# Constants first, rows in two parts, modulation tiles interleaved one pair ahead, and all four early column groups multiplied directly in fp32

## The chip, the cores and the metric

The kernel runs on one core of one Trainium2 chip. The metric is the device time of one execution in microseconds (us). The core has a tensor engine (PE, whose weight loads are listed as PEld), a vector engine (DVE), a scalar engine (ACT), GpSimd (POOL) and a sync engine (SP). Each of them takes its own instructions in order; they wait for one another through semaphores only. Transfers between HBM and on-chip memory are issued by SP, ACT and POOL and carried by 16 DMA engines.

## The reference

Two transformer-like blocks over 256 positions and width 2048, all in fp32. What matters here is how the first block begins:

```
mod = silu(c) @ w_ada + b_ada                 # 2048 -> 12288, one row
sh_a, sc_a, gt_a, sh_f, sc_f, gt_f = split(mod, 6)
h = rmsnorm(x, g_pre_attn) * (1 + sc_a) + sh_a
proj = h @ w_in                               # 2048 -> 6144: qa ka va qb kb vb
qa, ka, qb, kb = rope(...)                    # two attentions, then w_out
x = x + gt_a * rmsnorm(mix @ w_out)
# gated feed-forward, then the second block (mLSTM + convolution), a final norm
```

The projection can't begin before the row `mod` is known for the columns of `h` that it uses, and `mod` is itself a product with a large matrix (`w_ada`), done on the vector engine.

## The kernel before, in words

**Streamed weights.** All weights come as chunks of 1 MB, 128 partitions of 8 KB, into `RAW`, a ring of four slots (`RAWS = 4`). There are two kinds. A chunk of kind "A" holds the columns of `w_ada` for 128 values of `mod`: DVE multiplies it with the broadcast row `silu(c)` and sums (`ada_chunk`, line 1586), and the slot is free. A chunk of kind "W" holds two halves of 1024 columns of a projection. SP issues the loads in the order of the list that `first_body` returns, and before each it waits until the chunk four places earlier has been consumed (`slot_wait`).

**Halves.** A half, numbered h, is multiplied with one pair of k-tiles (2 x 128 rows of the contraction) of the activations for one group of 512 output columns. In the usual way ("split") ACT writes a rounded high part `HI` (line 648), DVE writes the rest `LO = RAW - HI` (line 1576), and PE makes 12 matmuls of 512 columns in the fp32r format: `XH*HI`, `XL*HI` (lines 1175, 1176) and `XH*LO` (line 1184). In the "direct" way ACT copies the raw half to `WHOLE` (line 645), DVE only writes one word so that the semaphore order stays (line 1573), and PE makes 4 matmuls of 512 columns in full fp32 with the unsplit `XT` (line 1199). Before, only group 3 of the first four groups is direct.

**The beginning.** Halves 0 to 31 are the first four column groups (`EARLY = 4`), walked k-pair by k-pair: for each of the eight pairs n, four A chunks give shift and scale of its two k-tiles, `first_scale(n)` (line 1815) finishes them, ACT's `x_pair(n)` (lines 763, 764) modulates `XT` and rounds to `XH`, DVE's `x_low(n)` (line 1821) makes `XL`, and then two W chunks hold the pair's four halves, one for each group. From half 32 on groups are walked one after the other, each with all eight pairs, always split; the attention's rotations, scores and products stand between the halves at places written out by hand (`ROPE_AT`, `QK_TURN_AT`). From chunk 18 on an A chunk follows nearly every W chunk. The other sections (feed-forward, down projection, second block) follow in the same ring.

**Start.** ACT issues the row `c` and five small loads (positions, `INV`, `COL`, `BCOL`, `IDENT`), SP the first A chunk and all of `x` as one transfer. ACT sums the squares of both row tiles (line 680), normalizes both (lines 743, 744), PE turns them with `IDENT` (line 1244), ACT copies them to `XT` (line 747). DVE computes the rotation angles (`angles`, lines 1790 to 1802) between the third and the fourth A chunk.

Of the kernel before, what the change touches and what calls it, by code (L numbers as in the profile page):

```python
# [348 lines left out]
def build(nc, x, c_rows, pos_cols, cols, bias_cols, lambda_q1, lambda_k1, lambda_q2, lambda_k2,  # L349
          b_in_2, normf_w_2, w_mod, w_first, w_ffn, w_down, w_second, w_gates, b_gates, k_ident, k_inv, k_mask_a, k_mask_b,  # L350
# [2083 lines left out]
```

## Time and profile before

| | us |
|---|---|
| median of 3 runs | 2419.84 |
| lowest, highest | 2418.53, 2421.32 |
| the profiled execution's own time | 2416.39 |
| its span | 2414.6 |
| PE busy | 2319.4 (96%) |
| DVE busy | 1828.0 (76%) |
| ACT busy | 1120.2 (46%) |

The profile is of one execution. The span runs from its first to its last recorded instruction; the time holds 1.8 us more around it. In all views "us" counts from the start of the span. Busy time of PE overlaps between pipelined matmuls; where PE is the bound, the distance from one start to the next is what counts. Records of a direct matmul appear twice (8 for the 4 matmuls of a half).

### The profile page before, as it was taken

The page shows a single profiled execution, that of the slowest core. Times are in us where ns is not written, and L with a number is a line of the kernel's source. Part 1 is how long each engine was busy: PE and PEld are TensorE (multiplying, and loading weights), DVE is VectorE, ACT ScalarE, POOL GpSimd, SP SyncE. Part 2 cuts the span into 40 slices and gives each one's busy share as a digit, 9 for nine tenths or more (in the row PEclk, how much of TensorE's full clock was granted, in tenths as well). Part 3 has the DMA queues.
Part 4 walks back from the last instruction along what each step waited for, and adds up shares of the span by engine and source line. Part 5 has one row for each costly group of instructions (what it writes and reads, how often), then busy time and mean ns, then how long its engine had stood idle before and what let it go on. Part 6 is the DMA issues. An engine that isn't in the chain of part 4 may idle for free.

```text
span 2414.6 us, 26091 instructions
## 1 busy us (share of the span) xinstructions
PE 2319.4 (96%) x10236; PEld 1898.1 (79%) x10236; DVE 1828.0 (76%) x2447; ACT 1120.2 (46%) x1470; POOL 16.7 (1%) x31
## 2 busy tenths in 40 slices
PE   4789999999999999999989999999999999999998
PEld 3557778778888888888868888888888888888887
DVE  5878988877878888887665567898778696555875
ACT  4334557465434444444464334444445544444453
POOL 0000000000000000000000000000000000000000
PEclk9899999999999999999989999999999999999999
DMA  8987788977788777888835655556566658555553
GB/s 314 363 322 268 279 295 334 367 266 286 276 251 327 279 280 279 302 331 318 300 137 190 231 190 197 176 203 205 205 202 206 208 196 252 208 192 192 192 192 122
DMA packets 88363, 599.51 MB, mean 248 GB/s; under 512 B 10416, under 2 KB 10816, under 8 KB 17072
## 3 DMA queue, kind: packets, MB, share of 16 engines
q1 hardware_dynamic: 85520, 588.94, 68.4%
q0 software_dynamic: 1712, 7.19, 0.9%
q8 instruction: 81, 1.33, 0.2%
q10 hardware_dynamic: 1008, 1.71, 0.2%
q14 instruction: 42, 0.34, 0.0%
HBM read 595.66 MB, written 2.13 MB: 248 GB/s over the span
## 4 chain that ended last, share of the span: by engine, by line
PE 87%; DVE 5%; DMA 3%; ACT 2%; issue 1%; DVEq 0%; ACTq 0%
PE PS L1159 20%; PE PS L1175 18%; PE PS L1184 18%; PE PS L1176 18%; PE PS L1164 10%; DMA RAW<-in_w_mod 2%; DVE RAW L1586 2%; DVE LO L1576 2%; DMA RAW<-in_w_first 1%; ACT HI L648 1%; PE PS L1290 1%; PE PS L1505 0%; ACT R L763 0%; DVE X L1663 0%; PE PS L1254 0%
## 5 line engine op out<-in xcount | busy, mean ns | idle before, releaser
L648 ACT ACTIVATE HI<-RAW 128x1024 fp32r<-128x1024 f32 x800 | 843.8, 1059 | 1109.9 <-PE PS L1184 659.3
L1576 DVE TENSOR_TENSOR LO<-RAW,HI 128x1024 fp32r<-128x1024 f32 x800 | 975.4, 1223 | 473.3 <-ACT HI L648 469.5
L1175 PE MATMUL PS<-HI,XH 128*128 128x512 f32 x2144 | 856.2, 399 | 37.1 <-ACT HI L648 28.1
L1176 PE MATMUL PS<-HI,XL 128*128 128x512 f32 x2144 | 843.3, 393 | 0.0
L1184 PE MATMUL PS<-LO,XH 128*128 128x512 f32 x2144 | 581.0, 392 | 0.3 <-DVE LO L1576 0.3
L1175 PEld LDWEIGHTS PS<-HI,XH 128*128 128x128 f32 x2144 | 407.2, 190 | 131.2 <-DVE XL L1821 33.7
L1184 PEld LDWEIGHTS PS<-LO,XH 128*128 128x128 f32 x2144 | 406.8, 190 | 87.3 <-DVE LO L1576 1.4
L1176 PEld LDWEIGHTS PS<-HI,XL 128*128 128x128 f32 x2144 | 407.8, 190 | 82.7 <-issue 0.2
L1159 PE MATMUL PS<-HI,XH 128*128 128x512 f32 x1056 | 326.3, 390 | 3.7 <-issue 2.3
L1159 PE MATMUL PS<-HI,XL 128*128 128x512 f32 x1056 | 325.9, 390 | 0.0
L1164 PE MATMUL PS<-LO,XH 128*128 128x512 f32 x1056 | 284.5, 390 | 0.0
L1614 DVE STREAM_TRANSPOSE R<-R 32x256 f32<-32x256 f32 (+1 forms) x608 | 230.9, 380 | 12.7
L1586 DVE CUSTOM_DVE_ANT_0 RAW<-RAW,BIAS 128x2048 f32<-128x2048 f32 x96 | 218.5, 2287 | 25.0 <-DMA RAW<-in_w_mod 13.5
L1159 PEld LDWEIGHTS PS<-HI,XH 128*128 128x128 f32 x1056 | 197.8, 188 | 44.8 <-issue 2.5
L1164 PEld LDWEIGHTS PS<-LO,XH 128*128 128x128 f32 x1056 | 198.8, 188 | 41.4
L1159 PEld LDWEIGHTS PS<-HI,XL 128*128 128x128 f32 x1056 | 198.5, 188 | 41.5
L1586 DVE CUSTOM_DVE_ANT_0 RAW<-RAW,R 128x2048 f32<-128x2048 f32 x48 | 109.9, 2289 | 0.5
L763 ACT ACTIVATE R<-R,MOD,SCALE 128x256 f32<-128x256 f32 x16 | 9.6, 599 | 80.2 <-DVE SCALE L1815 80.0
L1244 PE MATMUL PS<-IDENT,R 128*128 128x128 f32 x32 | 5.0, 332 | 28.5 <-DMA IDENT<-in_k_ident 28.5
L2234 DVE TENSOR_TENSOR R<-PS,BIAS 128x1024 f32<-128x1024 f32 x24 | 29.2, 1216 | 0.0
L1199 PE MATMUL PS<-R 128*128 128x512 f32 x64 | 28.7, 592 | 0.0
L1244 PEld LDWEIGHTS PS<-IDENT,R 128*128 128x128 f32 x32 | 4.8, 178 | 28.5 <-DMA IDENT<-in_k_ident 28.5
(246 smaller groups left out, 857.7 us busy)
## 6 DMA issues: line engine op xcount, KB each, us to landing
RAW<-in_w_second SPq DMA_DIRECT2D x208, 1024.0 KB, 4.8
RAW<-in_w_mod SPq DMA_DIRECT2D x144, 1024.0 KB, 5.8
RAW<-in_w_ffn SPq DMA_DIRECT2D x88, 1024.0 KB, 4.9
RAW<-in_w_first SPq DMA_DIRECT2D x64, 1024.0 KB, 6.5
RAW<-in_w_down SPq DMA_DIRECT2D x44, 1024.0 KB, 5.0
BIAS<-in_b_in SPq DMA_DIRECT2D x40, 256.0 KB, 5.2
R<-mod_rows POOLq DMA_DIRECT2D x3, 1024.0 KB, 9.8
X<-in_x SPq DMA_DIRECT2D x1, 2048.0 KB, 14.2
```

Of the source, the lines that this page charges most:

```text
L648: act.activation(HI[:, (it["half"] + hf) % HLS, :], whole, ACT.Copy).then_inc(s.hi_ready, 1)
L1159: pe.matmul(PS[:, bank_of(u, cc), :], x, HI[:, slot, cc * 512:(cc + 1) * 512], start=first and x is xh, stop=False)
L1164: m = pe.matmul(PS[:, bank_of(u, cc), :], XH[:, slot_k, u * P:(u + 1) * P], LO[:, slot, cc * 512:(cc + 1) * 512], start=False, stop=last)
L1175: pe.matmul(PS[:, bank + u, :], XH[:, 2 * n + kk, rows], hi, start=start and kk == 0, stop=False)
L1176: pe.matmul(PS[:, bank + u, :], XL[:, 2 * n + kk, rows], hi, start=False, stop=False)
L1184: m = pe.matmul(PS[:, bank + u, :], XH[:, 2 * n + kk, u * P:(u + 1) * P], lo, start=False, stop=stop and kk == 1)
L1199: m = pe.matmul(PS[:, bank + u, :], XT[:, 2 * n + kk, u * P:(u + 1) * P], as_it_is(h)[:, kk * 512:(kk + 1) * 512], start=start and kk == 0 ...
L1290: ins = pe.matmul(PS[:, 5, m * S:m * S + nk], QT[2 * m][rows, j, u * P:(u + 1) * P], QT[2 * m + 1][rows, j, 0:nk], start=True, stop=True, ...
L1576: dve.tensor_tensor(LO[:, slot, :], RAW[:, it["slot"], hf * 1024:(hf + 1) * 1024], HI[:, slot, :].bitcast(F32), ALU.subtract).then_inc(s.l ...
L1586: dve.tensor_tensor_reduce(w, w, C_ROW if a < ADA_OF_C else C_ROW_2, 1.0, 0.0, ALU.mult, ALU.add, MOD[:, a:a + 1]).then_inc(s.ada_step, 1)
L1614: m = dve.transpose(columns(b, a), rows(a, b))
L2234: dve.tensor_tensor(dst, y, bias, ALU.add).then_inc(s.group_out, 1)
```

## The change

It does six things.

1. `DIRECT` holds all four early groups: halves 0 to 31 all take the direct way. The four slots of `WHOLE` are now shared by four consecutive halves instead of four halves of group 3.
2. `first_body`: four A chunks, then for each pair n two A chunks of the next pair ahead of each of its two W chunks (none at the last pair).
3. `COL`, `BCOL`, `IDENT` and `INV` come as one tile `SMALLS`, issued first on ACT's queue; the row `c` moves from ACT's queue to the head of SP's.
4. `x` comes as two transfers; its squares start when the first has landed. Row tile 1 is normalized by DVE instead of ACT.
5. `angles` moves from behind the third A chunk to behind the fourteenth, `lambdas` from behind the sixth chunk of the list to behind the tenth A chunk, ACT's `tables` from half 5 to half 14.
6. PE's first two pairs of turns of rotated columns stand one half earlier.

```
-DIRECT = (3,)
+DIRECT = (0, 1, 2, 3)
...
-QK_TURN_AT = [(33, 34), (35, 36), (37, 38), (39, 40), (58, 60), (66, 68), (74, 76), (82, 84)]
+QK_TURN_AT = [(32, 33), (34, 35), (37, 38), (39, 40), (58, 60), (66, 68), (74, 76), (82, 84)]
...
 def first_body():
-    body = []
+
+    body = [("A",)] * 4
     for n in range(8):
-        body += [("A",)] * 4 + [("W", 2 * n), ("W", 2 * n + 1)]
+        ahead = [("A",)] * (2 if n < 7 else 0)
+        body += ahead + [("W", 2 * n)] + ahead + [("W", 2 * n + 1)]
...
+            sp.dma_start(C_ROW, c_rows[0:1, :].to_broadcast([P, D])).then_inc(s.c_in, 16)
...
                     if it["j"] == 0:
-                        sp.dma_start(X[:], x[0].rearrange("(u p) d -> p u d", p=P)).then_inc(s.x_in, 16)
+                        for u in range(NT):
+                            sp.dma_start(X[:, u, :], x[0, u * P:(u + 1) * P, :]).then_inc((s.x_in, s.x_in_1)[u], 16)
...
-            act.dma_start(C_ROW, c_rows[0:1, :].to_broadcast([P, D])).then_inc(s.c_in, 16)
+            act.dma_start(SMALLS[:], smalls).then_inc(s.small_in, 16)
             act.dma_start(POSI[:], pos_cols).then_inc(s.pos_in, 16)
-            act.dma_start(INV, k_inv.to_broadcast([P, 96])).then_inc(s.pos_in, 16)
-            act.dma_start(COL[:], cols).then_inc(s.small_in, 16)
-            act.dma_start(BCOL[:], bias_cols).then_inc(s.small_in, 16)
-            act.dma_start(IDENT[:], k_ident).then_inc(s.ident_in, 16)
...
-            act.activation(XN[:, 0, :], X[:, 0, :], ACT.Copy, scale=RSTD[:, 0:1])
-            act.activation(XN[:, 1, :], X[:, 1, :], ACT.Copy, scale=RSTD[:, 1:2]).then_inc(s.rows_normed, 1)
+            act.activation(XN[:, 0, :], X[:, 0, :], ACT.Copy, scale=RSTD[:, 0:1]).then_inc(s.rows_normed, 1)
...
-                if h == 5:
+                if h == 14:
                     tables()
...
-                    dve.memset(SMALL[:, 175:176], 0.0).then_inc(s.lo_ready, 1)
+                    dve.memset(READ[:, h:h + 1], 0.0).then_inc(s.lo_ready, 1)
...
                 dve.reciprocal(RSTD, ROOT).then_inc(s.rstd_ready, 1)
+                dve.wait_ge(s.rstd_ready, 1)
+                dve.tensor_scalar(XN[:, 1, :], X[:, 1, :], RSTD[:, 1:2], None, ALU.mult).then_inc(s.row_1, 1)
...
-                    if it["j"] == 1:
+                    if it["ada"] == 1:
+                        first_columns()
                         first_rstd()
-                    if it["j"] == 2:
+                    if it["ada"] == 13:
                         angles()
-                        first_columns()
...
-                    if it["j"] == 6:
+                    if it["ada"] == 9:
                         lambdas()
```

On the vector engine one pair in the middle of the beginning reads like this before (ISA with RAW is an A chunk, MEMSET the word of a direct half).

```order
L1586 ISA RAW,MOD<-RAW,BIAS 128x2048
L1586 ISA MOD 128x1
L1814 TENSOR_TENSOR MOD<-MOD,BCOL 128x4
L1815 SCALAR_TENSOR_TENSOR SCALE<-MOD,COL 128x2
L1821 TENSOR_TENSOR XL<-R,XH 128x512
L1576 TENSOR_TENSOR LO<-RAW,HI 128x1024 x3
L1573 MEMSET SMALL 128x1
L1586 ISA RAW,MOD<-RAW,BIAS 128x2048
```

And now, from the low part of a pair to the next one's.

```order
L1822 TENSOR_TENSOR XL<-R,XH 128x512
L1572 MEMSET READ 128x1 x2
L1585 ISA RAW,MOD<-RAW,BIAS 128x2048
L1585 ISA MOD 128x1
L1585 ISA RAW,MOD<-RAW,BIAS 128x2048
L1585 ISA MOD 128x1
L1815 TENSOR_TENSOR MOD<-MOD,SMALLS 128x4
L1816 SCALAR_TENSOR_TENSOR SCALE<-MOD,SMALLS 128x2
L1572 MEMSET READ 128x1 x2
L1585 ISA RAW,MOD<-RAW,BIAS 128x2048
```

The subtractions for LO are gone, and the scale of a pair no longer stands directly ahead of that pair's low part: two W halves, two A chunks and the next pair's work lie between.

On the sync engine the list of loads begins like this before (w_mod are the A chunks, w_first the W chunks).

```order
L543 DMA RAW<-in_w_mod 128x2048
L559 DMA X<-in_x 128x2x2048
L543 DMA RAW<-in_w_mod 128x2048 x3
L543 DMA RAW<-in_w_first 128x2048 x2
L543 DMA RAW<-in_w_mod 128x2048 x4
L543 DMA RAW<-in_w_first 128x2048 x2
```

And now.

```order
L554 DMA BIAS<-in_c_rows 128x2048
L544 DMA RAW<-in_w_mod 128x2048
L562 DMA X<-in_x 128x2048 x2
L544 DMA RAW<-in_w_mod 128x2048 x5
L544 DMA RAW<-in_w_first 128x2048
L544 DMA RAW<-in_w_mod 128x2048 x2
L544 DMA RAW<-in_w_first 128x2048
```

The row `c` stands at the head, and the first W chunk now comes after six A chunks instead of four.

On the tensor engine the beginning before repeats, eight times, three split halves and one direct; now it is the 32 turns of `x`, then 128 direct matmuls in one piece, and the first turn of rotated columns behind half 32.

```order
L1242 MATMUL PS<-SMALLS,R 128x128 x32
L1197 MATMUL PS<-R 128x512 x128
L1173 MATMUL PS<-HI,XH 128x512
L1174 MATMUL PS<-HI,XL 128x512
L1173 MATMUL PS<-HI,XH 128x512
L1174 MATMUL PS<-HI,XL 128x512
L1173 MATMUL PS<-HI,XH 128x512
L1174 MATMUL PS<-HI,XL 128x512
L1173 MATMUL PS<-HI,XH 128x512
L1174 MATMUL PS<-HI,XL 128x512
L1182 MATMUL PS<-LO,XH 128x512 x4
L1278 MATMUL PS<-SMALLS,R 128x128 x4
```

The last row is that turn; before, the first one stood behind half 33.

## Rows read from the trace of the kernel before

**Rows 1.** The page: busy time of PE, and PE in 40 slices.

```profile
PE 2319.4 (96%) x10236; PEld 1898.1 (79%) x10236; DVE 1828.0 (76%) x2447; ACT 1120.2 (46%) x1470; POOL 16.7 (1%) x31
...
PE   4789999999999999999989999999999999999998
```

**Rows 2.** Chain that ended last, pairs 6 and 7: start, us, what.

```profile
129.22 8.46 DMA RAW<-in_w_mod
...
140.43 0.61 ACT R L763
...
143.30 3.50 DVE LO L1576 x3
146.85 8.37 DMA RAW<-in_w_mod
```

**Rows 3.** Waits from 0 to 200 us: total, times, longest.

```profile
ACT R L763 <- DVE SCALE L1815: 80.0, 7, 12.2
PEld PS L1175 <- DVE XL L1821: 33.7, 7, 7.7
```

**Rows 4.** Windows: length, busy of each engine, PE clock, DMA share, GB/s.

```profile
0.00:10.00 10.00, 0.00 (x0) 0.00 (x0) 0.06 (x1) 1.64 (x2) 0.20 (x4) 1.00 0.82 302
10.00:20.00 10.00, 0.00 (x0) 0.00 (x0) 4.19 (x3) 7.05 (x7) 3.37 (x6) 1.00 0.97 389
20.00:30.00 10.00, 1.49 (x7) 1.49 (x8) 8.51 (x27) 4.10 (x3) 0.00 (x0) 1.00 1.00 318
...
135.00:140.00 5.00, 4.25 (x12) 1.87 (x10) 4.60 (x4) 0.00 (x0) 0.00 (x0) 1.00 1.00 421
140.00:145.00 5.00, 1.58 (x5) 1.31 (x6) 2.71 (x6) 4.50 (x6) 0.00 (x0) 0.89 1.01 424
145.00:150.00 5.00, 5.00 (x19) 4.00 (x18) 5.00 (x6) 1.11 (x2) 0.00 (x0) 0.77 0.69 234
...
450.00:500.00 50.00, 48.55 (x213) 39.59 (x212) 43.04 (x41) 22.39 (x33) 0.00 (x0) 1.00 0.96 367
```

**Rows 5.** Timeline of the start: start us, us, engine, line, op, idle before.

```profile
22.87 1.99 ACT L744 ACTIVATE R<-X,SMALL 128x2048 f32<-128x2048 f32 x1
23.75 0.17 DVE L1790 CAST SMALL<-POSI 128x2 f32<-128x2 int32 x1
28.52 5.03 PE L1244 MATMUL PS<-IDENT,R 128*128 128x128 f32 x32 [28.52 <-DMA IDENT<-in_k_ident]
29.69 2.28 DVE L1586 CUSTOM_DVE_ANT_0 RAW<-RAW,BIAS 128x2048 f32<-128x2048 f32 x1
34.78 2.00 ACT L648 ACTIVATE HI<-RAW 128x1024 fp32r<-128x1024 f32 x2
39.39 0.77 PE L1175 MATMUL PS<-HI,XH 128*128 128x512 f32 x1 [5.84 <-DVE XL L1821]
```

**Rows 6.** DVE groups by form: line, op, count, busy us, mean ns.

```profile
L1657 DVE TENSOR_SCALAR R<-X,SMALL 128x1024 f32<-128x1024 f32 x4 | 2.8, 748 | 0.0
```

**Rows 7.** Timeline of PE: starts of halves 29 and 30.

```profile
165.39 0.40 PE L1175 MATMUL PS<-HI,XH 128*128 128x512 f32 x1
...
168.12 0.39 PE L1175 MATMUL PS<-HI,XH 128*128 128x512 f32 x1
```

**Rows 8.** The chain at half 31, the last direct one.

```profile
171.00 3.43 PE PS L1199 x8
```

**Rows 9.** Timeline of DVE, PE, SP and ACT behind half 37.

```profile
190.36 0.69 DVE L1859 TENSOR_TENSOR R<-PS,R 128x512 f32<-128x512 f32 x1 [0.66 <-PE PS L1184]
...
196.46 1.09 PE L1279 MATMUL PS<-IDENT,R 128*128 128x128 f32 x4 [3.46 <-ACT R L776]
197.20 0.78 PE L1175 MATMUL PS<-HI,XH 128*128 128x512 f32 x1
...
198.68 0.33 SPq L543 DMA_DIRECT2D RAW<-in_w_first  x1
...
204.38 1.06 ACT L648 ACTIVATE HI<-RAW 128x1024 fp32r<-128x1024 f32 x1 [6.19 <-DMA RAW<-in_w_first]
```

More of the change, by code:

```diff
@@ L346, in turned_at, with build @@
     return (g, part) if 0 <= g < 11 else None
[L349 to L350 removed]
+def build(nc, x, c_rows, pos_cols, smalls, lambda_q1, lambda_k1, lambda_q2, lambda_k2,
+          b_in_2, normf_w_2, w_mod, w_first, w_ffn, w_down, w_second, w_gates, b_gates, k_mask_a, k_mask_b,
           k_mask_m, out):
@@ L369, in build @@
         X = sb("X", [P, NT, D])
-        IDENT = sb("IDENT", [P, P])
-        COL = sb("COL", [P, 146])
+        SMALLS = sb("SMALLS", [P, 514])
+        COL, BCOL, IDENT, INV = SMALLS[:, 0:146], SMALLS[:, 146:290], SMALLS[:, 290:418], SMALLS[:, 418:514]
         COL2 = COL[:, 96:114]
         MOD = sb("MOD", [P, ADA_CHUNKS])
-        BCOL = sb("BCOL", [P, ADA_CHUNKS])
         SCALE = sb("SCALE", [P, NK])
@@ L382, in build @@
         WIFL = sb("WIFL", [P, NK, 16], F32R)
+        READ = sb("READ", [P, 8 * EARLY])
         POSI = sb("POSI", [P, NT], I32)
@@ L603, in gate_rows @@
                 pool.dma_start(rows, v.to_broadcast([P, D])).then_inc(s.gg_in, 16)
-            pool.wait_ge(s.x_in, 16)
+            pool.wait_ge(s.x_in_1, 16)
             for n, v in enumerate((lambda_q1, lambda_k1, lambda_q2, lambda_k2)):
@@ L676, in squares @@
                 for u in range(NT):
+                    act.wait_ge((s.x_in, s.x_in_1)[u], 16)
                     if u:
@@ L1256, in turn_pair @@
                 m.then_inc(s.pair_t, 1)
-            pe.wait_ge(s.ident_in, 16)
+            pe.wait_ge(s.small_in, 16)
+            pe.wait_ge(s.row_1, 1)
             pe.wait_ge(s.rows_normed, 1)
@@ L1777, in first_columns @@
             def first_columns():
-                dve.wait_ge(s.small_in, 32)
+                dve.wait_ge(s.small_in, 16)
                 dve.tensor_copy(MIXC[:, 0:1], COL2[:, 16:17])
@@ L2396, in laid_out, with inverse_frequencies @@
             "c_rows": np.concatenate([np.asarray(inputs[n]).reshape(1, D) for n in ("c", "c_2")]), "pos_cols": np.asarray(inputs["positions"]).reshape(NT, P).T,
-            "cols": columns(*(inputs[n] for n in ("g_pre_attn", "g_pre_ffn", "norm1_w_2", "conv_w_2", "headnorm_w_2", "g_out_a",
+            "smalls": np.concatenate([columns(*(inputs[n] for n in ("g_pre_attn", "g_pre_ffn", "norm1_w_2", "conv_w_2", "headnorm_w_2", "g_out_a",
                                                   "g_subln_b", "g_post_attn", "g_post_ffn"))),
-            "bias_cols": in_turn(b_ada, b_ada_2).T}
+                                      in_turn(b_ada, b_ada_2).T, np.eye(P), np.repeat(inverse_frequencies(), P, axis=0)],
+                                     axis=1).astype(np.float32)}
+def inverse_frequencies():
+    return np.concatenate([(np.float32(10000.0) ** (-np.arange(n, dtype=np.float32) / np.float32(n))).astype(np.float32)
+                           for n in (HD // 2, QKD // 2)])[None, :]
 def constants():
@@ L2413, in constants @@
     mask_m = np.concatenate([later[0:P, :], later[0:P, 0:P]], axis=1).astype(np.float32)
-    inv = [(np.float32(10000.0) ** (-np.arange(n, dtype=np.float32) / np.float32(n))).astype(np.float32)
-           for n in (HD // 2, QKD // 2)]
-    return {"k_ident": np.eye(P, dtype=np.float32), "k_inv": np.concatenate(inv)[None, :], "k_mask_a": halves(mask_a),
+    return {"k_mask_a": halves(mask_a),
             "k_mask_b": halves(mask_b), "k_mask_m": mask_m}
```

6 lines of the change are left out of this document (2 added, 4 removed).

## The prediction, made before the changed kernel ran

> **What bounds the kernel now.** I first read the page. PE is busy for 96% of the span, so outside its idle stretches nothing but less work on PE can help. The 40 slices say where the idle is: the first three slices (0 to 180 us) read 4, 7, 8, nearly all others 9 [rows 1]. The change touches only what runs up to about 200 us, and behind it every load waits for a slot and every slot for an engine, so a gain made by half 32 is carried to the end unchanged. So the question is when half 32 starts: now at 174.4 us, the end of half 31's chain piece (171.00 + 3.43) [rows 8].
>
> Next the chain of waits in that stretch. It isn't a chain through PE. For each pair it goes DMA (8.4 us), an A chunk on DVE, modulation on ACT, three LO subtractions (3.5 us), DMA again; two links of the same kind are 17.63 us apart (129.22 to 146.85) [rows 2]. The waits agree: ACT waits 80 us for SCALE, PE 34 us for XL [rows 3]. The loop is closed by the ring: the next A chunks can be loaded only when the W chunks are consumed, these wait for the modulation, and this for the last A chunk. What to see in the windows: while the chain is in its DMA link, the transfers run at 421 to 424 GB/s; behind it they fall to 234 because the ring is full of W chunks that nobody may touch [rows 4]. Six chunks of 1.049 MB in 17.63 us are 357 GB/s.
>
> **The interleaving and the direct halves.** A pair still needs six chunks. With the modulation one pair ahead, a W chunk that lands can be copied at once (1.0 us a half) and its slot is free about 2 us after landing, as for an A chunk (2.3 us) [rows 5]. Then the loop is open and the longest of three loads per pair sets the pace. PE: a split half takes 2.73 us (165.39 to 168.12) [rows 7], a direct one 3.43 [rows 8]; three of four halves change, +2.1 us a pair, from 11.6 to 13.7 us. This is 8 x 2.1 = 16.8 us more work on PE, and it costs nothing only while PE waits for chunks anyway. DVE: minus three LO (3.5 us), leaving four A chunks (9.1), the low part and the scale (about 1), 10.2 us. DMA: six chunks at 424 GB/s take 14.8 us, at the 367 GB/s that the stretch from 450 to 500 us shows at a share of 0.96 they take 17.1 [rows 4]. So DMA is the next bound, PE 1 us behind it. I take 410 GB/s, 15.3 us a pair: the new stretch has the same mix of A and W chunks on the same queue as the windows at 421 to 424 and is nearest to them, but short dips remain whenever DVE stands behind a W chunk.
>
> The page "DMA: Bandwidth & Descriptors" of the Trainium skill, section "Where 436 GB/s comes from", gives about 358 GB/s as what one core gets from HBM and says that this side binds for such loads. By it the pace would stay 17.6 us a pair and the interleaving would bring nothing. The 5-us windows above it speak against that rule here; it is a rival below.
>
> **Half 32 by counting bytes.** By 30 us the core has moved 3.0 + 3.9 + 3.2 = 10.1 MB [rows 4], and I leave that as it is: the same bytes are asked for, in another order. In the new order chunk W13 is the last behind which no A chunk stands; up to it go 32 A, 14 W, `c` and `x` (3), 49 transfers or 51.4 MB, with 1.0 MB of small ones 52.4. The other 42.3 MB at 410 GB/s take 103.2 us: W13 lands at 133.2. The angles (from 23.75 to the next A chunk at 29.69 on DVE [rows 5], 5.9 us) now stand between the fourteenth A chunk and the third pair's low part. For some 1.6 us of them DVE would have waited for a W chunk's copy anyway. The ring has some 2.2 us of slack: four slots at 2.55 us are 10.2, of which 5.7 go from issue to landing (198.68 to 204.38) [rows 9] and 2.3 to DVE. I charge the rest, 2.1 us: 135.3. From there a copy (1.1 us) and six direct halves, 6 x 3.43 = 20.6 us: half 32 starts at 157.0, **17.4 us earlier**. Bounds: 424 GB/s and nothing for the angles gives 151.5 (22.9 earlier); 367 GB/s gives 169 (5.4 earlier).
>
> **The start.** PE's turns begin at 28.52, when IDENT lands, though the rows are ready at 24.9 (22.87 + 1.99); then 34.78 for the first copy and 39.39 for the first half [rows 5]. With SMALLS first the turns need only the rows. Normalizing tile 1 on DVE beside ACT is 2 x 748 ns less a fixed part, about 1.3 us [rows 6], and saves ACT 2.0. So turns start near 23.3, 5 us earlier, and XT is ready near 29.4. But the first W chunk now comes seventh among the chunks and waits for the slot of the third (free near 24.6); with 5 us to land behind two queued chunks it lands near 32. Two copies, the modulation and the low part put half 0 near 37, only 2.5 us earlier. As W13's landing and not half 0 sets half 32, the start is worth **0** in the sum; without the DMA cover (PE as the bound) it would be worth these 2.5 us. Putting `c` at the head of SP's queue delays the first chunk by about 2.5 us and `c` comes some 3 us earlier: also 0.
>
> **The turns.** The rotation of group 2 waits for both turns of group 0, that of group 3 for both turns of group 1; group 3's starts at 190.36 and behind it stand an A chunk and LO of halves 38, 39, whose end lets SP load W21 at 198.68, which lands at 204.38 [rows 9]. One half earlier (3.2 us with its turn) moves this sequence by about 3.3 us against half 32. PE reaches the wait for W21 sooner too: 24.5 us behind half 32's start while the chunk's copy and the evacuation are done at 28.1, a pause of 3.6 us. Just such a pause (3.46 us) stands before 196.46, and behind it the first matmul record lasts 0.78 instead of 0.39 us [rows 9]: the granted clock is at the lower of its two levels (1.2 against 2.4 GHz), which takes about 2 us over a half. So 3.3 less up to 2: I take **2.0**, bounds 1.3 to 3.3. Tables, lambdas, READ: 0, they stand beside DMA waits.
>
> **Sum.** 17.4 + 2.0 = 19.4 us off the profiled execution's 2416.4 (span 2414.6 and 1.8 around it). That execution lies 3.4 under the median of 2419.8; against the median the forecast is **2400.4 us**.
>
> **The rivals.**
> - *PE becomes the bound.* If the chunks come at 424 GB/s or more, the direct passes bite: half 0 at 37, about 2.4 us for the lower clock of its beginning, 32 x 3.43 = 109.8: half 32 at 149.2. With 2.0 that is 27.2 off: 2392.6. For it: PE's load of 13.7 is only 1.1 under DMA's 14.8. Against: it needs a ring that is never empty.
> - *DMA doesn't go faster.* Sustained loads run at 358 to 375 GB/s, the windows at 424 being bursts after a pause. Pace 16.8 to 17.6 us a pair, W13 at 143 to 148 without the angles, half 32 at 166 to 172: 4 to 10 off, 2410 to 2416. For it: 367 over 50 us at a share of 0.96, and the rule of the page. Against: two neighbouring windows at 421 and 424 [rows 4].
> - *The change does only in part what it says.* Direct halves use XT only, yet PE still waits for XL at each pair's first half, and DVE makes it in its order behind A chunks and one-word writes that wait for copies. If that binds in each pair and not only at the angles, 1 us a pair: 10 to 14 off, 2406 to 2410.
> - *Slower: the clock.* If the direct stretch, with a short wait before each W chunk, ran at the lower level, a half would take 6.86 us, 27.4 a pair, half 32 would start at 37 + 219 = 256, 82 us late: 2500. Decisive from the point where more than about a quarter of the stretch is at that level (13.7 x 1.27 = 17.4). For it: the clock falls in each pair now (0.77 in 145 to 150) [rows 4]. Against: it falls behind pauses of 4 us and more, and the new pauses are 1 to 2 us, split in two.
>
> **How the numbers follow.** Forecast (2396 to 2406) 0.50; PE bound (2392 to 2396) 0.17; DMA no faster 0.20, a quarter of it within 0.2% (4.8 us, about what a measurement of this kernel can tell from no change); XL binds 0.08; clock 0.05. Faster 0.90, same 0.05, slower 0.05. The range for 8 in 10 is 2393 to 2412: it leaves out the clock, the upper third of "no faster" and the lower end of "PE bound", some 0.18.
>
> **What would show it.** In the new profile: half 32's first split matmul at 157 (152 to 169); the distance of two scales near 15.3 us (17.6 if DMA is no faster, 13.7 to 14 if PE is the bound); DMA near 410 GB/s from 40 to 130 us without dips to 234; no waits of ACT for SCALE; direct halves 3.43 us apart within a chunk; turns at 23 us, half 0 near 37; the granted clock at 1.00 behind 45 us. The forecast is wrong if the ring runs dry although DVE and ACT are ahead, or if PE's waits behind half 32 grow by as much as the start gained.

## The result, and the profile after

The changed kernel takes **2401.9 us** (median of 4 runs, 2401.3 to 2404.6); the kernel before, run beside it, 2420.6 (4 runs, 2418.5 to 2421.9). The ratio is 0.9926 with an interval of 0.9909 to 0.9943: 17.9 us faster (13.8 to 22.0). The forecast was 19.4 us faster, 2400.4. The profiled execution took 2404.6 us (span 2402.8), the highest of its four, while that of before (2416.4) lies under its own median. So the two traces lie only 11.8 us apart where the medians lie 18.6 apart (the ratio gives 17.9). Read traces for places, medians for the total.

The page of the kernel after, span, busy time and slices (40 slices of 60 us):

```profile
span 2402.8 us, 25898 instructions
...
PE 2329.6 (97%) x10140; PEld 1876.0 (78%) x10140; DVE 1803.0 (75%) x2448; ACT 1119.8 (47%) x1469; POOL 16.7 (1%) x31
...
PE   4999999999999999999989999999999999999998
```

Where [rows 1] read 4, 7, 8 stands now 4, 9, 9. PE is busy for 10.2 us more (2319.4 to 2329.6) although the whole is shorter. Direct halves cost more than split ones; the forecast had 16.8 us for that, and less of the span runs at the lower clock now (mean granted clock 0.990 against 0.987), which fits with the rest.

Windows of the kernel after, one of 30 us, one of 20 and then 10 each (length, busy of PE, PEld, DVE, ACT, POOL, PE clock, DMA share, GB/s), to compare with [rows 4]:

```profile
0.00:30.00 30.00, 5.71 (x32) 5.49 (x32) 11.18 (x17) 14.88 (x14) 3.56 (x10) 1.00 0.92 330
30.00:50.00 20.00, 10.55 (x20) 4.70 (x21) 14.01 (x18) 7.55 (x10) 0.00 (x0) 0.74 0.99 396
...
60.00:70.00 10.00, 9.29 (x22) 3.80 (x20) 8.43 (x19) 4.01 (x6) 0.00 (x0) 1.00 1.01 424
70.00:80.00 10.00, 7.74 (x18) 3.53 (x19) 9.22 (x19) 3.84 (x5) 0.00 (x0) 1.00 0.85 324
80.00:90.00 10.00, 10.00 (x25) 4.41 (x24) 7.25 (x8) 2.00 (x2) 0.00 (x0) 1.00 1.01 420
90.00:100.00 10.00, 9.99 (x24) 4.14 (x22) 4.72 (x9) 9.11 (x12) 0.00 (x0) 1.00 0.94 359
100.00:110.00 10.00, 8.41 (x19) 3.63 (x20) 6.05 (x13) 2.38 (x3) 0.00 (x0) 1.00 0.95 385
110.00:120.00 10.00, 9.58 (x23) 4.10 (x22) 7.62 (x9) 3.35 (x5) 0.00 (x0) 1.00 1.02 426
120.00:130.00 10.00, 9.75 (x23) 4.10 (x22) 7.54 (x11) 3.75 (x6) 0.00 (x0) 1.00 1.01 422
```

The falls to 234 GB/s in every pair are gone. Two dips are left: 324 behind the angles and 359 and 385 around the tables. Everything else from 50 to 140 us runs at 418 to 426, at a granted clock of 1.00 in this profile.

Waits of the kernel after from 0 to 200 us (total, times, longest), to compare with [rows 3]:

```profile
ACT R L648 <- DMA RAW<-in_w_first: 64.9, 14, 7.8
DVE RAW L1585 <- DMA RAW<-in_w_mod: 25.7, 22, 9.2
...
PE PS L1197 <- DVE XL L1822: 15.2, 3, 11.2
```

ACT's 80 us of waiting for SCALE have become waits for transfers, and PE's 33.7 us for XL have shrunk to 15.2, of which 11.2 are the start. The loop is open and the bound is DMA, as forecast, with PE close behind: from half 0 to half 32 it pauses for 6.6 us in all.

Timeline of PE in the kernel after (start, us, engine, line, op, count, idle before and what ended it), to compare with [rows 5, 7, 8]:

```profile
22.54 5.71 PE L1242 MATMUL PS<-SMALLS,R 128*128 128x128 f32 x32 [22.54 <-ACT R L742]
39.45 29.84 PE L1197 MATMUL PS<-R 128*128 128x512 f32 x64 [11.20 <-DVE XL L1822]
72.26 27.73 PE L1197 MATMUL PS<-R 128*128 128x512 f32 x64 [2.97 <-DVE XL L1822]
...
139.24 20.87 PE L1197 MATMUL PS<-R 128*128 128x512 f32 x48 [0.95 <-ACT R L648]
```

Half 32 follows at 139.24 + 20.87 = 160.1 us: 14.3 earlier than the 174.4 of before.

### The profile page after: what moved, and what is told of

The parts are those of the page before. It is cut to its first block, busy times and chain, and to the rows that moved or that the text cites. A ratio compares the mean times of both kernels' runs of the same rounds, so it can differ in the third digit from the quotient of the medians.

```text
span 2402.8 us, 25898 instructions
## 1 busy us (share of the span) xinstructions
PE 2329.6 (97%) x10140; PEld 1876.0 (78%) x10140; DVE 1803.0 (75%) x2448; ACT 1119.8 (47%) x1469; POOL 16.7 (1%) x31
## 4 chain that ended last, share of the span: by engine, by line
PE 89%; DMA 5%; DVE 4%; issue 1%; ACT 1%; DVEq 0%; SPq 0%; ACTq 0%
PE PS L1157 20%; PE PS L1173 19%; PE PS L1174 18%; PE PS L1182 18%; PE PS L1162 10%; DMA RAW<-in_w_mod 3%; DMA RAW<-in_w_first 2%; DVE RAW L1585 2%; PE PS L1197 1%; PE PS L1289 1%; DVE LO L1575 0%; PE PS L1504 0%; DVE X L1662 0%; PE PS L1252 0%; ACT HI L651 0%
## 5 line engine op out<-in xcount | busy, mean ns | idle before, releaser
L651 ACT ACTIVATE HI<-RAW 128x1024 fp32r<-128x1024 f32 x776 | 820.0, 1059 | 1111.1 <-PE PS L1182 666.1
L1575 DVE TENSOR_TENSOR LO<-RAW,HI 128x1024 fp32r<-128x1024 f32 x776 | 947.2, 1223 | 471.3 <-ACT HI L651 467.5
L1173 PE MATMUL PS<-HI,XH 128*128 128x512 f32 x2048 | 813.6, 397 | 2.4 <-DVE XL L1683 2.0
L1174 PE MATMUL PS<-HI,XL 128*128 128x512 f32 x2048 | 801.8, 392 | 0.0
L1182 PE MATMUL PS<-LO,XH 128*128 128x512 f32 x2048 | 551.6, 390 | 0.3 <-DVE LO L1575 0.3
L1182 PEld LDWEIGHTS PS<-LO,XH 128*128 128x128 f32 x2048 | 385.7, 188 | 82.0 <-DVE LO L1575 1.0
L1174 PEld LDWEIGHTS PS<-HI,XL 128*128 128x128 f32 x2048 | 386.9, 189 | 78.4 <-issue 0.2
L1157 PE MATMUL PS<-HI,XH 128*128 128x512 f32 x1056 | 326.9, 391 | 3.5 <-issue 2.3
L1157 PE MATMUL PS<-HI,XL 128*128 128x512 f32 x1056 | 326.1, 390 | 0.0
L1162 PE MATMUL PS<-LO,XH 128*128 128x512 f32 x1056 | 284.8, 390 | 0.0
L1162 PEld LDWEIGHTS PS<-LO,XH 128*128 128x128 f32 x1056 | 198.8, 188 | 41.5
L1157 PEld LDWEIGHTS PS<-HI,XL 128*128 128x128 f32 x1056 | 198.7, 188 | 41.5
L1197 PE MATMUL PS<-R 128*128 128x512 f32 x256 | 114.0, 604 | 17.8 <-DVE XL L1822 15.2
L1197 PEld LDWEIGHTS PS<-R 128*128 128x128 f32 x256 | 48.8, 193 | 82.5 <-issue 69.9
L648 ACT ACTIVATE R<-RAW 128x1024 f32<-128x1024 f32 x32 | 32.1, 1048 | 66.6 <-DMA RAW<-in_w_first 64.9
## 6 DMA issues: line engine op xcount, KB each, us to landing
X<-in_x SPq DMA_DIRECT2D x2, 1024.0 KB, 11.8
```

Of the source, the lines that this page charges most:

```text
L648: act.activation(as_it_is(h), whole, ACT.Copy).then_inc(s.hi_ready, 1)
L651: act.activation(HI[:, (it["half"] + hf) % HLS, :], whole, ACT.Copy).then_inc(s.hi_ready, 1)
L1157: pe.matmul(PS[:, bank_of(u, cc), :], x, HI[:, slot, cc * 512:(cc + 1) * 512], start=first and x is xh, stop=False)
L1162: m = pe.matmul(PS[:, bank_of(u, cc), :], XH[:, slot_k, u * P:(u + 1) * P], LO[:, slot, cc * 512:(cc + 1) * 512], start=False, stop=last)
L1173: pe.matmul(PS[:, bank + u, :], XH[:, 2 * n + kk, rows], hi, start=start and kk == 0, stop=False)
L1174: pe.matmul(PS[:, bank + u, :], XL[:, 2 * n + kk, rows], hi, start=False, stop=False)
```

## The landmarks

The experiments are read at four places of each trace: the start of half 32, the first weight load of a later stretch of the attention (line 1310 after, 1311 before), the last one of line 1340 (1341 before), and the span. In e1 and e3 these lines stand a few lines lower. Each number is from that kernel's timeline.

| kernel | half 32 | half 32 to first 1310 | first 1310 to last 1340 | span | time, median |
|---|---|---|---|---|---|
| before, first profile | 174.4 | 52.4 | 200.1 | 2414.6 | 2420.6 |
| before, again | 174.3 | 54.6 | 200.7 | 2416.1 | 2422.1 |
| after, first profile | 160.1 | 51.4 | 203.6 | 2402.8 | 2401.9 |
| after, again | 159.5 | 50.2 | 203.3 | 2401.4 | 2403.2 |
| e1 direct only | 167.4 | 52.0 | 202.0 | 2409.3 | 2412.7 |
| e2 change less the new direct halves | 161.4 | 50.6 | 204.8 | 2402.8 | 2406.0 |
| e3 old start | 156.0 | 50.6 | 202.2 | 2397.8 | 2400.7 |
| e4 old turns | 161.3 | 52.2 | 204.2 | 2404.0 | 2403.1 |
| e5 third turns | 160.9 | 47.2 | 202.8 | 2399.2 | 2400.9 |
| e6 tables late | 157.7 | 50.5 | 203.1 | 2402.0 | 2402.8 |
| e7 angles late too | 154.6 | 51.3 | 202.4 | 2397.2 | 2398.3 |
| e8 no wait for low part | 159.7 | 50.5 | 204.8 | 2403.6 | 2404.6 |
| e9 combined | 154.0 | 46.3 | 203.6 | 2390.9 | 2392.5 |

The kernel before took 2419.3 to 2419.4 us beside each of the three groups of runs (7 to 13 runs each).

Up to half 32 the changed kernel, its second profile, e4 and e5 are the same program. They have half 32 at 159.5, 160.1, 160.9 and 161.3 us. So this landmark scatters by 1.8 us between executions, and a single profile must be held against all four.

## Experiments: which part brings the gain

**The change again**, beside e1 to e3 on one chip.

> The changed kernel once more, beside the other three and with a second profile. The two profiled executions at hand differ by 11.8 us, the medians by 18.6. If the gain of 15.3 us that stands at half 41 is carried to the end and the rest is scatter between executions, this profile shows half 32 at 160.1 us again and a span near 2400. If the seams at 315 and 405 us always give 3.5 us back, the span is 2402 to 2403 again and the pauses there last 3.5 us and more.

Measured: 2403.2 us, ratio 0.9935 (0.9918 to 0.9953), 16.2 us faster. Together with the first result the gain is 16 to 18 us. Half 32 stands at 159.5, and the span of 2401.4 lies between the two outcomes that the expectation named.

**e1: the direct halves alone**, on the kernel before. The order of loads, the start and the turns stay.

```
-DIRECT = (3,)
+DIRECT = (0, 1, 2, 3)
...
-                    dve.memset(SMALL[:, 175:176], 0.0).then_inc(s.lo_ready, 1)
+                    dve.memset(READ[:, h:h + 1], 0.0).then_inc(s.lo_ready, 1)
```

> The kernel before with all four early groups direct, the order of the chunks as before. My theory: the loop of DMA, A chunk, modulation and release stays closed; the three LO subtractions (3.5 us a pair) leave it, copies on ACT take part of their place, so a pair takes about 16 instead of 17.6 us and half 32 starts 6 to 10 us earlier: 2411 to 2415. Rival: the direct halves cost on PE what they add, 0.7 us each for 24 halves: up to 16.8 us slower, 2437.

Measured: 2412.7 us, ratio 0.9976 (0.9966 to 0.9985), 6.7 faster. Half 32 starts 7.0 earlier. Timeline of DVE in e1, the scales of neighbouring pairs:

```profile
100.44 0.16 DVE L1816 SCALAR_TENSOR_TENSOR SCALE<-MOD,COL 128x2 f32<-128x2 f32 x1
116.41 0.16 DVE L1816 SCALAR_TENSOR_TENSOR SCALE<-MOD,COL 128x2 f32<-128x2 f32 x1
132.47 0.16 DVE L1816 SCALAR_TENSOR_TENSOR SCALE<-MOD,COL 128x2 f32<-128x2 f32 x1
```

The pace is 16.0 us a pair against 17.6: the three subtractions left the loop, but the loop is still closed (windows from 60 to 120 us between 341 and 429 GB/s). PE's 16.8 us of extra work did not show: the time fell.

**e2: the change without the new direct halves.** It is the changed kernel with groups 0 to 2 split again. Besides the order it keeps the new start, the moved one-off work and the new turns, so it isn't the order alone.

```
-DIRECT = (0, 1, 2, 3)
+DIRECT = (3,)
```

> The changed kernel with group 3 alone direct, everything else as changed. My theory: the interleaving opens the loop by itself; DVE then has about 13.9 us a pair, under DMA's 14.9, and behind chunk W13 PE has 17.8 instead of 20.6 us up to half 32. So 0 to 3 us faster than the changed kernel, 2399 to 2402. Rival: the low parts hold the W slots so long that the ring runs dry: 5 to 12 us slower than the changed kernel.

Measured: 2406.0 us, ratio 0.9947 (0.9926 to 0.9967), 13.4 faster than before and 2.8 slower than the changed kernel beside it. The expectation, as fast or faster, was missed, and so was its rival (5 us and more slower). Windows of e2:

```profile
60.00:70.00 10.00, 7.97 (x20) 4.84 (x20) 7.75 (x15) 5.35 (x7) 0.00 (x0) 0.83 1.02 428
70.00:80.00 10.00, 5.38 (x14) 4.16 (x14) 9.58 (x18) 2.39 (x3) 0.00 (x0) 0.67 0.54 205
80.00:90.00 10.00, 10.00 (x38) 6.98 (x37) 9.36 (x13) 3.84 (x5) 0.00 (x0) 0.99 1.00 412
```

Split halves do save PE work, which is worth nothing while DMA is the bound, and they load DVE: 9.4 us of 10 in the last of these windows against 7.3 in the changed kernel. So the angles, 5.9 us of DVE, cut a hole down to 205 GB/s instead of 324, and PE's clock falls in it. What the direct halves buy in the new order is slack on DVE: ACT copies chunk W13 at 142.2 us in e2 and at 137.5 to 139.3 in the four profiles of the new beginning. The quicker halves behind it give most of that back, and half 32 starts at 161.4. So no more than 2 of the 2.8 us are lost ahead of half 32; e2 also has one of the longest stretches from line 1310 to 1340 (204.8). The parts do not add up (6.7 and 13.4 against 16.2 for all), as is to be expected of two changes that shorten the same loop.

**e3: the old start with the new order.** It is e1 with the new list of loads, the new turns (its expectation speaks of the old ones, the kernel has the new) and `lambdas` behind the sixth A chunk. The constants, `x` in one transfer, the angles behind the third chunk and the tables at half 5 are as before.

```
-QK_TURN_AT = [(33, 34), (35, 36), (37, 38), (39, 40), (58, 60), (66, 68), (74, 76), (82, 84)]
+QK_TURN_AT = [(32, 33), (34, 35), (37, 38), (39, 40), (58, 60), (66, 68), (74, 76), (82, 84)]
...
+    body = [("A",)] * 4
     for n in range(8):
-        body += [("A",)] * 4 + [("W", 2 * n), ("W", 2 * n + 1)]
+        ahead = [("A",)] * (2 if n < 7 else 0)
+        body += ahead + [("W", 2 * n)] + ahead + [("W", 2 * n + 1)]
...
-                    if it["j"] == 6:
+                    if it["ada"] == 5:
```

> The kernel before with all four early groups direct and the new order of chunks alone: constants, c, x, the normalization, angles and tables at their old places, lambdas behind the sixth A chunk, turns as before. The prediction put the new start at 0 and charged the moved angles with 2.1 us; the trace shows two dips of DMA (at 70 and 90 us) behind the moved angles and tables, together some 4 us. Theory: half 32 starts 2 to 4 us earlier than in the changed kernel, less 1 for the turns: 2398 to 2402. Rival: the new start is what keeps the first chunks flowing, and without it half 32 is 3 us and more later: 2405 and above.

Measured: 2400.7 us, ratio 0.9921 (0.9903 to 0.9939), 2.4 under the changed kernel beside it. Half 32 starts at 156.0, 3.5 earlier than there. Windows of e3:

```profile
50.00:60.00 10.00, 10.00 (x25) 4.40 (x24) 7.40 (x11) 6.03 (x8) 0.00 (x0) 1.00 1.01 425
...
70.00:80.00 10.00, 10.00 (x25) 4.41 (x24) 7.30 (x11) 3.72 (x5) 0.00 (x0) 1.00 1.02 422
...
90.00:100.00 10.00, 9.98 (x24) 4.30 (x23) 6.22 (x10) 4.99 (x7) 0.00 (x0) 1.00 1.01 420
```

No window from 50 to 140 us lies under 419. Half 32 comes 3.5 to 5.3 us earlier than in the four profiles of the changed kernel's beginning, with the old start. The likely cause is the place of the angles and tables, which in the changed kernel is inside the stretch paced by DMA; e6 and e7 test that alone. What the new start is worth by itself no pair of runs shows. The nearest is e3 against e7, which has the new start and the one-off work behind the stretch: by 50 us e7 has moved 18.1 MB and e3 17.5, and e7's half 32 comes 1.4 us earlier. This may be the start or e3's early angles and tables.

## Experiments: what the one-off work costs, and where

**e6: the tables at half 28** in the changed kernel, where ACT has nothing to hold up.

```
-                if h == 14:
+                if h == 28:
                     tables()
```

> The changed kernel with ACT's two table loads and three activations (91.5 to 94.8 us) at half 28 instead of 14, where ACT waits for PE anyway. The prediction put them at 0. Theory: they hold back the copy of half 15, with it DVE's next A chunks by 4.3 us and the ring by about 2: without them the dip of DMA between 90 and 110 us (359 and 385 GB/s) goes and half 32 starts 1.5 to 2.5 us earlier than at 160.1. Rival: they stand beside DMA, and half 32 doesn't move.

Measured: the windows of e6 where the changed kernel has 359 and 385:

```profile
90.00:100.00 10.00, 10.00 (x25) 4.43 (x24) 6.00 (x13) 5.73 (x7) 0.00 (x0) 1.00 1.01 423
100.00:110.00 10.00, 10.00 (x25) 4.25 (x24) 7.24 (x10) 3.73 (x5) 0.00 (x0) 1.00 1.01 422
```

Half 32 starts at 157.7, 1.8 to 3.6 earlier than in the four profiles. By 50 us e6 has moved 18.05 MB and they 17.75 to 17.98, which is 0.2 to 0.7 us of it; about 2.2 us are left for the tables. The time, 2402.8 us (ratio 0.9926, 0.9907 to 0.9946), can't be told from the changed kernel's. The mechanism stands on four lines of the changed kernel, ACT, DVE and SP (its issues):

```profile
90.25 0.33 SPq L544 DMA_DIRECT2D RAW<-in_w_first  x1
...
91.47 1.28 ACT L749 ACT_TABLE_LOAD   x1
...
95.88 2.29 DVE L1585 CUSTOM_DVE_ANT_0 RAW<-RAW,BIAS 128x2048 f32<-128x2048 f32 x1 [4.30 <-issue]
...
95.99 2.54 SPq L544 DMA_DIRECT2D RAW<-in_w_mod  x2
```

The tables stand between the two halves of one W chunk's copy. DVE writes its word for that chunk only behind the copy, so it stands still for 4.3 us ahead of an A chunk that it could have taken, no slot comes free, and SP issues nothing from 90.6 to 96.0.

**e7: the angles and `lambdas` behind the last A chunk too.**

```
-                    if it["ada"] == 13:
-                        angles()
...
-                    if it["ada"] == 9:
+                    if it["ada"] == 31:
+                        angles()
                         lambdas()
```

> As the last, and DVE's angles and lambdas moved from behind the fourteenth and tenth A chunk to behind the thirty-second, where DVE idles. Theory: no dip of DMA is left from 30 to 130 us (420 GB/s throughout), W13 lands near 133.5 and half 32 starts at 155 to 156.5, 4 us earlier than in the changed kernel: 2397 to 2400. It tests the prediction's 2.1 us for the angles. Rival: the dips are of DMA's own, or the angles late hold up the first rotations: half 32 not before 158, or DVE late at half 34.

Measured: 2398.3 us, ratio 0.9909 (0.9885 to 0.9933), and half 32 at 154.6, another 3.1 earlier (one profile each; both had moved 18.1 MB by 50 us, and by 90 us e7 is 1.3 MB ahead, which is 3.0 us). Windows of e7:

```profile
70.00:80.00 10.00, 10.00 (x25) 4.50 (x24) 7.44 (x11) 3.73 (x5) 0.00 (x0) 1.00 1.01 419
80.00:90.00 10.00, 10.00 (x24) 4.37 (x24) 5.97 (x13) 4.14 (x5) 0.00 (x0) 1.00 1.01 422
```

So the two placements together cost the changed kernel 5 us or a little more at half 32 (4.9 to 6.7 by its four profiles), 3.1 for the angles with `lambdas`, which moved along, and about 2.2 for the tables.

**e8: PE waits for the high part only.** A direct half uses neither XH nor XL. Here it waits for XH, written just behind `XT` by ACT, and only half 32 waits for all low parts.

```
                     if g == 0:
-                        pe.wait_ge(s.x_ready, n + 1)
+                        pe.wait_ge(s.xh_ready, n + 1)
+                    if h == 8 * EARLY:
+                        pe.wait_ge(s.x_ready, 8)
```

> The changed kernel with PE waiting for XH instead of XL at the first half of each early pair, and for all of XL at half 32 (direct halves don't read XL). The prediction had a rival in which this wait binds in each pair (1 us a pair). Theory: it binds only at half 0 (0.7 us) and behind the angles (the pause of 3.0 us before 72.3), and there DMA sets the pace anyway: half 32 at 159.5 to 160.2, time as the changed kernel within 1 us. Rival: PE's lead frees WHOLE slots and chunks earlier: half 32 2 us and more earlier.

Measured: 2404.6 us, ratio 0.9939 (0.9924 to 0.9954), half 32 at 159.7. PE no longer stops at 72 us, and stops later instead (8.03 us busy of 80 to 90, at a clock of 0.83), since the chunks come no sooner. Half 32 lies inside the scatter of the changed kernel's profiles (159.5 to 161.3) and the time 1.4 to 2.7 us above its two medians, where the expectation had it within 1. Taking the wait for XL away gains nothing; that rival falls.

## Experiments: behind half 32

**e4: the turns as before.**

```
-QK_TURN_AT = [(32, 33), (34, 35), (37, 38), (39, 40), (58, 60), (66, 68), (74, 76), (82, 84)]
+QK_TURN_AT = [(33, 34), (35, 36), (37, 38), (39, 40), (58, 60), (66, 68), (74, 76), (82, 84)]
```

> The changed kernel with the turns of rotated columns at their old places (33, 34), (35, 36). The prediction gave the earlier turns 2.0 us (1.3 to 3.3), the trace 15.3 - 14.3 = 1.0. Theory: the third group's rotation, the A chunk, the low parts of halves 38 and 39 and the load of W21 come 3.3 to 3.7 us later against half 32; PE's pause moves to behind half 37, as in the kernel before, and what was 1.0 is lost: 2404 (1 us over the changed kernel). Rival: DVE is so idle between halves 32 and 36 now that the earlier turns bring nothing: same.

Measured: from half 32 to line 1310 it takes 52.2 us, against 50.2 and 51.4 in the two profiles of the changed kernel: the turns are worth 1 to 2 us. One profile would not carry that, but all of them together do: the four with the old turns (both of before, e1, e4) have 52.0 to 54.6, the seven with the changed kernel's turns 50.2 to 51.4. PE's pause moved to behind half 37 as expected (3.18 us before 183.1), with a second one of 1.53 before 192.8. By the time they can't be measured (2403.1 us, ratio 0.9928, 0.9905 to 0.9952).

Why not more is to be seen in the changed kernel, PE and ACT behind half 39, which answer [rows 9]:

```profile
186.41 1.06 ACT L651 ACTIVATE HI<-RAW 128x1024 fp32r<-128x1024 f32 x1 [6.29 <-DMA RAW<-in_w_first]
...
188.09 1.09 PE L1278 MATMUL PS<-SMALLS,R 128*128 128x128 f32 x4 [3.27 <-ACT R L774]
188.83 0.78 PE L1173 MATMUL PS<-HI,XH 128*128 128x512 f32 x1
189.41 0.63 PE L1174 MATMUL PS<-HI,XL 128*128 128x512 f32 x1
189.83 0.63 PE L1173 MATMUL PS<-HI,XH 128*128 128x512 f32 x1
...
194.03 0.60 PE L1278 MATMUL PS<-SMALLS,R 128*128 128x128 f32 x4
```

Chunk W21 is at ACT 18.0 us earlier than before (204.38), 3.6 more than half 32. But PE gets there early as well, pauses for 3.27 us, and then runs at the lower level (starts 0.425 us apart instead of 0.235): from this turn to the next (194.03) it takes 5.9 us instead of the 3.2 that it takes ahead of the pause. At that turn (before at 209.28) 15.3 us of the lead remain.

**e5: the third pair of turns one half earlier too.**

```
-QK_TURN_AT = [(32, 33), (34, 35), (37, 38), (39, 40), (58, 60), (66, 68), (74, 76), (82, 84)]
+QK_TURN_AT = [(32, 33), (34, 35), (36, 37), (39, 40), (58, 60), (66, 68), (74, 76), (82, 84)]
```

> The changed kernel with the third pair of turns one half earlier too, at (36, 37). In the changed kernel PE pauses 3.3 us before the turn behind half 39 because ACT writes out the turn before it only behind its copy of W21, and then runs a half at the lower clock (5.2 instead of 2.8 us). Theory: with both turns of group 2 written out ahead of W21's copy the pause and the slow half go: 5 to 6 us less between half 32 and half 41, 2397 to 2399. Rival: the pause only moves, to the first half that needs W21 (half 42): 0 to 2 us.

Measured: 2400.9 us, ratio 0.9916 (0.9897 to 0.9935). Timeline of PE in e5:

```profile
180.01 0.63 PE L1278 MATMUL PS<-SMALLS,R 128*128 128x128 f32 x4 [0.36 <-ACT R L774]
180.40 0.48 PE L1173 MATMUL PS<-HI,XH 128*128 128x512 f32 x1
...
190.60 0.63 PE L1278 MATMUL PS<-SMALLS,R 128*128 128x128 f32 x4 [1.26 <-ACT R L774]
```

The pause of 3.27 us and the slow half behind it are gone; pauses of 0.36 and 1.26 us stand in their place and the granted clock is 1.00 in every window from 50 to 200 us. From half 32 to line 1310 it takes 47.2 us, 3 to 4 less, where 5 to 6 were expected; 1.26 us of the difference is the second pause. The time lies 1.0 to 2.3 us under the changed kernel's two medians and above the 2397 to 2399 expected.

**The kernel before again.** Is the 203 us that the changed kernel needs for the stretch from line 1310 to 1340, where before needed 200.1, the scatter of one execution?

> The kernel before as a run of its own, for a second profile. Up to half 41 all profiles of changed kernels keep their gain, from there to the end of the attention (first L1310 record to last L1340 record, 200.1 us in the one profile of before) they take 202.8 to 204.8. Theory: that one execution (2416.4, below the median of 2419.4) met short pauses by luck, and a second takes 202 to 204 too, with half 32 at 174.4 again; then nothing of the gain is given back. Rival: before takes 200 again, and a gain at the beginning always costs 3 us at the seams.

Measured: 2422.1 us (ratio 1.0007, 0.9995 to 1.0019), and the stretch takes 200.7 us. The eleven profiles of changed kernels have 202.0 to 204.8, the two of the changed kernel itself 203.6 and 203.3. My expectation, that before would come out like them, was wrong: **2.6 to 3.5 us of what the beginning gains is given back there** (1.3 to 4.7 over all eleven). Waits of PE from 150 to 460 us, first of the kernel before (its second profile), then of the changed one:

```profile
PE PS L1311 <- issue: 2.9, 1, 2.9
PE PS L1341 <- ACT R L827: 2.6, 2, 1.5
```

```profile
PE PS L1310 <- issue: 3.5, 1, 3.5
...
PE PS L1340 <- ACT R L825: 3.0, 1, 3.0
```

The other two profiles have 2.4 and 2.3 us (before, the first) and 3.7 and 4.1 (the changed kernel, the second). Windows, of before's first profile over the whole stretch, of the changed kernel's first over the stretch and at line 1340, and of its second at line 1340:

```profile
226.80:426.90 200.10, 194.50 (x943) 157.98 (x942) 173.14 (x312) 128.93 (x313) 1.73 (x2) 0.99 0.85 303
...
211.50:415.10 203.60, 196.16 (x943) 159.70 (x942) 174.41 (x315) 129.11 (x313) 1.73 (x2) 0.98 0.85 302
...
408.00:413.00 5.00, 4.42 (x20) 4.12 (x20) 3.04 (x7) 3.94 (x11) 0.00 (x0) 0.66 0.96 344
...
408.00:413.00 5.00, 4.84 (x31) 4.36 (x32) 4.15 (x6) 4.29 (x11) 0.00 (x0) 1.00 1.00 374
```

The pauses and the clock account for all of it. PE idles for 5.6 and 6.4 us of the stretch in the two profiles of before, for 7.4 and 8.7 in those of the changed kernel. All four have one piece at the lower clock near line 1310, 3.4 us long (0.66 over 5 us), and the changed kernel's first profile has a second one of that size at line 1340. By an estimate from these rows such a piece costs half its length, 1.7 us. Without pauses and lower clock all four stretches are 192.7 to 192.9 us. So 1 to 3 us go in longer pauses and, in one of the two profiles, 1.7 in the clock. Why the pauses are longer stays open.

**e9: what the others point to.** It is e7 with the third turns earlier and the last pair's halves (28 to 31) split, since behind the last A chunk PE is the bound and DVE has time.

```
-    return h < 8 * EARLY and first_half(h)[0] in DIRECT
+    return h < 7 * EARLY and first_half(h)[0] in DIRECT
...
-QK_TURN_AT = [(32, 33), (34, 35), (37, 38), (39, 40), (58, 60), (66, 68), (74, 76), (82, 84)]
+QK_TURN_AT = [(32, 33), (34, 35), (36, 37), (39, 40), (58, 60), (66, 68), (74, 76), (82, 84)]
```

> The changed kernel with what the runs point to: angles and lambdas behind the thirty-second A chunk, tables at half 28, the third pair of turns at (36, 37), and halves 28 to 31 split again, since behind the last A chunks PE is the bound and DVE idles (4 x 0.7 = 2.8 us). Theory: half 32 near 152 (160 in the changed kernel), the pause and slow half behind 39 gone (3.6): 2403.2 - 8 - 3.6 = 2391.5, 2389 to 2394. Rival: the low parts of the last pair come behind the angles and hold up PE or the first rotation, and no more than the 5 us of the late angles stay: 2396 and above.

Measured: **2392.5 us**, ratio 0.9889 (0.9872 to 0.9905): 26.8 us under the kernel before and 9 to 11 under the changed one's two medians. Timeline of PE in e9:

```profile
135.97 7.13 PE L1197 MATMUL PS<-R 128*128 128x512 f32 x16 [0.63 <-ACT R L648]
...
173.06 0.63 PE L1278 MATMUL PS<-SMALLS,R 128*128 128x128 f32 x4 [0.34 <-ACT R L774]
```

The last direct half ends at 143.1, half 32 starts near 154.0, and line 1310 comes 46.3 us behind it. From 90 to 140 us its DMA ran at 409 to 425 GB/s, a little under e3's 419 to 424, and half 32 comes only 0.6 us ahead of e7's although four halves cost 2.8 us less. The rest went ahead of them: W13 is copied at 134.9 (e7 at 132.6), although the two programs do the same up to there, so this is scatter between executions. The time came out as expected (2389 to 2394), its parts did not: half 32 was expected near 152, and the stretch from there to line 1310 gained 4 to 5 us instead of 3.6.

## Why the prediction was right, step by step

**What bounds the kernel: right.** The closed loop was the bound, and opening it handed the bound to DMA. e1 shows the loop closed with less in it (16.0 us a pair), e2 and the changed kernel show it open.

**The rate: right in kind, taken a little low.** I took 410 GB/s and 15.3 us a pair. Without the one-off work the windows hold 419 to 428 (e3, e7) and two scales of the changed kernel are 14.9 us apart. Timeline of DVE:

```profile
122.57 0.16 DVE L1816 SCALAR_TENSOR_TENSOR SCALE<-MOD,SMALLS 128x2 f32<-128x2 f32 x1
...
137.48 0.16 DVE L1816 SCALAR_TENSOR_TENSOR SCALE<-MOD,SMALLS 128x2 f32<-128x2 f32 x1
```

The rival "DMA doesn't go faster" falls: e7 holds 419 to 428 GB/s in all eight windows from 50 to 130 us, so those before were no bursts. These windows go against the rule of about 358 GB/s that the prediction cited from the Trainium skill ("DMA: Bandwidth & Descriptors", section "Where 436 GB/s comes from"). Another page of the Trainium skill, "HBM Reference", section "Specifications (TRN2)", takes 358 GB/s as each core's share while both cores of a pair load, and about 425 GB/s for a core that streams alone. This trace agrees with the second part (419 to 428); no run here loads from two cores.

**Half 32: 17.4 forecast, 14.3 measured.** W13 was forecast to be there at 135.3 and is copied at 138.1 (137.5 to 139.3 in the four profiles). Timeline of ACT:

```profile
138.13 2.00 ACT L648 ACTIVATE R<-RAW 128x1024 f32<-128x1024 f32 x2 [6.14 <-DMA RAW<-in_w_first]
```

Two terms are off. The angles were charged 2.1 us and cost 3.1 (e6 to e7). The tables were put at 0 "beside DMA waits" and cost about 2.2 (e6): that was the step that failed. ACT's waiting time was read as free time, but the tables stand in the middle of a chunk's copy, and behind the copy queue DVE's word, an A chunk and SP's next load. The rate taken low by 3% hid these two terms: 42.3 MB at 422 GB/s instead of 410 take 3.0 us less, and the two add 1.0 and 2.2. What made W13 late against the forecast is then in the byte count. By 50 us the changed kernel has moved 17.8 MB (30 us at 330 and 20 at 396 GB/s), where 10.1 MB and 20 us at 422 would make 18.5: 1.8 us. And by 138.1 us it has moved 53.0 MB, 0.6 more than the 52.4 counted, since loads behind W13 are under way too: 1.4 us. So the 2.8 us are a balance of misses in both directions. Behind W13 six halves took 20.87 us against 20.6.

**The start: 0 in the sum, though half 0 gained nothing either.** Turns at 22.54 (23.3 forecast), W0 at ACT at 34.84 (32), half 0 at 39.45 (37 forecast, before 39.39): the turns start 6 us earlier and the first half doesn't, because W0 comes 2.8 us later than thought. Tile 1 on DVE took 1.28 us (1.3). e3 with the old start is no slower, but no pair of runs isolates the start, and up to 1.4 us at half 32 may belong to it (e3 against e7).

**The turns: 2.0 forecast, 1.0 in the changed kernel's trace** (15.3 at line 1278 against 14.3 at half 32), 1 to 2 by e4 and the profiles beside it. The forecast pause (3.6 us; 3.27 measured) and the lower clock behind it came; the clock's price was 2.7 us (5.9 less 3.2) and not 2.

**"Carried to the end unchanged": not quite.** 2.6 to 3.5 us of it go in the next stretch, in longer pauses and in one profile at the lower clock. So the first two traces lie 14.3 + 1.0 - 3.5 = 11.8 us apart, the second two 14.7, where the sum said 19.4. **That the median came out within 1.5 us of 2400.4 is in part luck.** The forecast subtracted its 19.4 from the profiled execution, which gives 2397.0, and the profiled execution after took 2404.6. Both profiled executions of before lie low: all 47 runs of that kernel have a median of 2419.4, and its profiles took 2416.4 and 2417.9; the eight runs of the changed kernel have 2403.0, its profiles 2404.6 and 2403.3. So 2 to 5 us of the 16.4 between these medians are in no pair of traces. One place where executions of before differ is seen: its second profile has a further pause of 2.56 us before 206.8, with the lower clock behind it, and takes 54.6 instead of 52.4 us from half 32 to line 1311. Whether its usual execution loses the rest there too stays open.

**The other rivals.** PE as the bound: not reached in the changed kernel, nearly in e7, where PE pauses for 1.4 us in all between half 0 (39.2) and half 32 (154.6). With no pause half 32 would start at 153.2; the rival's 149.2 had half 0 at 37. XL as the bound: refuted by e8. The clock: 1.00 in every window of the changed kernel's first profile from 50 to 150 us, and 0.83 in one of the second (70 to 80), so it never set the pace. But the argument against it was wrong. It said that the clock falls behind pauses of 4 us and more, while its own [rows 9] have it behind 3.46 us, and here it fell behind 2.01 us too. Window of the changed kernel's second profile:

```profile
70.00:80.00 10.00, 8.02 (x15) 3.55 (x16) 8.87 (x17) 3.84 (x5) 0.00 (x0) 0.83 0.85 305
```

## What to carry to other kernels

An engine that waits half of its time can still hold up a stream: look where in its order the one-off work stands, and what queues behind the instruction that it delays. Put such work where the stream has ended (e7); ahead of the stream it did no harm to the windows from 50 us on either (e3). Once a loop through a ring is opened, the slack of the engines that free its slots decides how deep a disturbance cuts; taking work off such an engine can pay though it is not the bound.
